# Attention's 16 own keys of each stream as a full block of 128 rows, padded with zeros

## The reference, cut to what matters

```python
ckv_all = jnp.concatenate([past_ckv.astype(c_kv.dtype), c_kv], axis=1)   # 256 + 16 keys
...
p = jax.nn.softmax(s, axis=-1).astype(v.dtype)
return jnp.einsum('bhqk,bkhd->bqhd', p, v)
```

## Time and profile before

| what | before |
|---|---|
| median of 3 runs | 1081.33 us (1079.39 to 1082.06) |
| span of the profiled execution | 1080.6 us |
| mean granted TensorE clock | 0.969 |
| PE busy | 1018.8 us (94%) |
| DVE busy | 760.0 us (70%) |
| ACT busy | 605.0 us (56%) |
| POOL busy | 82.3 us (8%) |

### The profile page before, as it was taken

How to read it: one execution, slowest core, us unless ns; L and a number is a source line. 1 busy time by engine, 2 the same in 40 slices (tenths; PEclk the granted TensorE clock), 3 DMA queues, 4 the chain that set the end, 5 groups by cost and what they waited for, 6 DMA issues and landing times.

```text
span 1080.6 us, 13540 instructions
## 1 busy us (share of the span) xinstructions
PE 1018.8 (94%) x5133; PEld 758.1 (70%) x5133; DVE 760.0 (70%) x645; ACT 605.0 (56%) x507; POOL 82.3 (8%) x109
## 2 busy tenths in 40 slices
PE   4999999999999999999969998989997989998997
PEld 4889998887666666666648686877785667766664
DVE  4456656267699888888815556662766999989896
ACT  5337432244577777777524233443536868887881
POOL 4000000004000000000021020000030000000003
PEclk9999999999999999999979999897898999999999
DMA  9542523684899999999366010303668999999984
GB/s 344 164 166 87 217 78 125 249 346 159 297 389 380 396 382 407 385 405 379 129 232 194 0 42 22 135 1 126 264 239 300 387 394 380 392 402 405 409 345 175
DMA packets 56923, 278.95 MB, mean 258 GB/s; under 512 B 6336, under 2 KB 10848, under 8 KB 48288
## 3 DMA queue, kind: packets, MB, share of 16 engines
q1 hardware_dynamic: 45424, 240.21, 57.7%
q0 software_dynamic: 8992, 29.74, 8.1%
q10 hardware_dynamic: 2464, 8.39, 2.0%
HBM read 260.45 MB, written 18.04 MB: 258 GB/s over the span
## 4 chain that ended last, share of the span: by engine, by line
PE 63%; issue 16%; DVE 8%; DMA 7%; ACT 3%; POOL 1%; ACTq 0%; SPq 0%; POOLq 0%; DVEq 0%
PE ps L189 19%; PE ps L195 9%; PE ps L527 4%; PE ps L581 4%; DMA raw<-in_moe_w_dram 4%; PE ps L624 3%; PE ps L1367 3%; PE ps L1364 3%; PE ps L2120 3%; PE ps L587 2%; PE ps L535 2%; DVE moe_wl L1104 2%; DVE raw_lo L1104 2%; PE ps L631 2%; PE ps L2095 1%
## 5 line engine op out<-in xcount | busy, mean ns | idle before, releaser
L1104 DVE TENSOR_TENSOR raw_lo<-raw,moe_wh 128x4096 fp32r<-128x4096 f32 x48 | 212.0, 4422 | 37.4 <-ACT moe_wh L1099 37.4
L1104 DVE TENSOR_TENSOR moe_wl<-moe_raw,moe_wh 128x4096 fp32r<-128x4096 f32 x48 | 212.0, 4422 | 33.6 <-ACT moe_wh L1099 33.4
L1099 ACT ACTIVATE moe_wh<-raw 128x4096 fp32r<-128x4096 f32 x48 | 174.0, 3625 | 20.8 <-DMA raw<-in_moe_w_dram 9.0
L1099 ACT ACTIVATE moe_wh<-moe_raw 128x4096 fp32r<-128x4096 f32 x48 | 173.9, 3624 | 14.1 <-DMA moe_raw<-in_moe_w_dram 14.1
L189 PE MATMUL ps<-moe_wh,moe_x 128*72 128x512 f32 x512 | 125.8, 398 | 1.7 <-DVE moe_x L1234 1.5
L189 PEld LDWEIGHTS ps<-moe_wh,moe_x 128*72 128x72 f32 x512 | 71.8, 143 | 46.0 <-DVE moe_x L1234 2.6
L329 DVE TENSOR_TENSOR raw_lo<-raw,gm_wh 128x4096 fp32r<-128x4096 f32 x12 | 53.1, 4424 | 69.6 <-ACT gm_wh L323 67.2
L189 PE MATMUL ps<-moe_wh,moe_hTh 128*72 128x512 f32 (+1 forms) x256 | 83.7, 410 | 4.9 <-DVE moe_hTl L1239 3.1
L189 PE MATMUL ps<-moe_wh,moe_hTl 128*72 128x512 f32 (+1 forms) x256 | 81.8, 401 | 0.0
L323 ACT ACTIVATE gm_wh<-raw 128x4096 fp32r<-128x4096 f32 x11 | 39.9, 3626 | 57.7 <-DMA raw<-in_gm_w_out_dram 29.2
L1364 PE MATMUL ps<-moe_wh,moe_x 128*128 128x512 f32 x224 | 58.9, 402 | 9.7 <-DVE moe_x L1234 9.7
(11 more groups left out here) (408 smaller groups left out, 1730.1 us busy)
## 6 DMA issues: line engine op xcount, KB each, us to landing
raw<-in_moe_w_dram SPq DMA_DIRECT2D x48, 2048.0 KB, 11.6
moe_raw<-in_moe_w_dram SPq DMA_DIRECT2D x48, 2048.0 KB, 11.9
raw<-in_gm_w_in_dram SPq DMA_DIRECT2D x7, 2048.0 KB, 7.9
raw<-in_gm_w_out_dram SPq DMA_DIRECT2D x4, 2048.0 KB, 7.6
moe_yrows<-moe_rows ACTq DMA_DIRECT2D x16, 288.0 KB
moe_rows<-moe_xrows POOLq DMA_DIRECT2D x14, 288.0 KB, 9.4
moe_rows<-moe_xrows POOLq DMA_DIRECT2D x14, 256.0 KB, 9.1
moe_yrows<-moe_rows ACTq DMA_DIRECT2D x14, 256.0 KB
```

The lines of the kernel that those rows point to most:

```text
L1099: nc.scalar.activation(w_hi[hi][:], w_raw[slot], ACT.Copy).then_inc(wh_ready, 1)
L1104: nc.vector.tensor_tensor(w_lo[slot], w_raw[slot], w_hi[hi][:].bitcast(F32), ALU.subtract).then_inc(wl_ready, 1)
```

## The change

`c_own` moves to partitions 112 to 127 of the same tile and gets 128 rows, of which POOL sets the first 112 to zero by a memset behind its DMAs. The third transpose turns the last 128 columns of the probabilities, that is 112 of cached keys and the 16 own ones, and ACT copies all three blocks at once. The 112 probabilities that come twice meet rows of zeros. The counts of `sm_pTc` are halved with the copies, and PE waits once for `own_zeroed`.

```diff
-        c_own = work[0:DECS, 2:4].rearrange("k a n -> k (a n)").rearrange("k (b r) -> k b r", b=DECB)
+        c_own = work[:, 2:4].rearrange("k a n -> k (a n)").rearrange("k (b r) -> k b r", b=DECB)
...
-                g.dma_start(c_own[:, b], c_sb[b * DECS:(b + 1) * DECS, SAMPLE, 0:KVR]).then_inc(ld_own, 16)
+                g.dma_start(c_own[P - DECS:P, b], c_sb[b * DECS:(b + 1) * DECS, SAMPLE, 0:KVR]).then_inc(ld_own, 16)
+            nc.gpsimd.memset(c_own[0:P - DECS], 0.0).then_inc(own_zeroed, 1)
...
-                nc.scalar.activation(psT[:, b % 2, 0:KC], ps[:, 2 + b % 2, 0:KC], ACT.Copy).then_inc(sm_pTc, 1)
-                nc.scalar.activation(psT[0:DECS, b % 2, KC:KC + P], ps[0:DECS, 2 + b % 2, KC:KC + P], ACT.Copy).then_inc(sm_pTc, 1)
+                nc.scalar.activation(psT[:, b % 2, 0:KC + P], ps[:, 2 + b % 2, 0:KC + P], ACT.Copy).then_inc(sm_pTc, 1)
...
             pe.wait_ge(ld_own, 16 * DECB)
+            pe.wait_ge(own_zeroed, 1)
...
-                    pe.wait_ge(sm_pTc, 2 * b - 2)
+                    pe.wait_ge(sm_pTc, b - 1)
...
-                nc.tensor.transpose(ps[0:DECS, 2 + b % 2, KC:KC + P], s_sb[:, b, KC:KALL], ident).then_inc(sm_pT, 1)
+                nc.tensor.transpose(ps[:, 2 + b % 2, KC:KC + P], s_sb[:, b, KALL - P:KALL], ident).then_inc(sm_pT, 1)
...
-                pe.wait_ge(sm_pTc, 2 * b + 2)
+                pe.wait_ge(sm_pTc, b + 1)
...
-                        probs = psT[0:DECS if c == 2 else P, b % 2, c * P:(c + 1) * P]
+                        probs = psT[:, b % 2, c * P:(c + 1) * P]
```

More of the change, by code:

```diff
@@ L1597, in build @@
             sem, ["sm_s", "sm_maxd", "sm_expd", "sm_p", "sm_pT", "sm_pTc", "sm_pc", "sm_pcc"])
-        sm_new, ld_own = sem("sm_new"), sem("ld_own")
+        sm_new, ld_own, own_zeroed = sem("sm_new"), sem("ld_own"), sem("own_zeroed")
         sm_o, pads_zeroed = sem("sm_o"), sem("pads_zeroed")
```

## The result

| | before | after |
|---|---|---|
| median of 6 runs each, same chip | 1080.74 us (1079.39 to 1082.20) | 1073.50 us (1072.69 to 1074.71) |
| span of the profiled execution | 1080.6 us | 1071.0 us |
| mean granted TensorE clock | 0.969 | 0.973 |

What follows compares the result with a forecast made beforehand. PE's path to the end of L2332, a gate for later loads and engines, was taken as the bound. Gaps and copy 3.0 us plus clock 1.8 gave 4.8: 1081.33 - 4.8 = 1076.5 us, range 1074.0 to 1080.5.

Steps and rivals of the forecast that it cites:

- The gaps: In values(b), changes between 16 and 128 rows cost PE 0.75 us; 1.50 us saved in streams 0, 4, 1.50 in 6, 7.
- DVE's idle time: Ahead of L1843, DVE's waits of 1.69 and 1.83 us were to fall by about 0.75 us each.
- the copy: Before values(6), ACT's one copy of 0.49 us replaces two, some 0.53 us in all: 0.04 us sooner.
- the memset: On POOL, zeroing 2048 columns on 112 partitions ends long before its first use: 0 us.
- The clock: From values(6) to the projection, a shorter stretch at half clock adds 1.8 us to the gain.
- 13.6: Length in us of the half-clock stretch before the change, 730.6 to 744.2 us, from values(6) almost to L2332.
- L: Length of the half-clock stretch after the change: expected 6.8 to 10 us, taken as 10.
- Rival 2: The half-clock stretch near stream 6 vanishes: gain 9.8 us, time 1071.5 us; chance 0.06.
- Streams 1, 2, 3 and 5 for nothing: In these streams DVE is the bound, so time saved on PE becomes idle time: 0 us.
- Rival 1: The half-clock stretch stays as long as it was: only 3.0 us gained, 1078.3 us; chance 0.20.
- rival 3: Row count doesn't matter, or time gained before L2332 is absorbed behind it: 1081.3 us; chance 0.12.
- Rival 4: The clock also falls mid-loop, a second half-clock stretch costing 6.8 us: slower, 1085.1 us; chance 0.07.

Runs made afterwards that it cites:

- the one profile with all gaps at the full clock: The kernel before with five dummy products in PE's pauses around stream 6, all gaps kept: 1081.11 us, ratio 0.9996; stage 45.4 us.
- the two later sets: Before and after measured again, no edit: 1080.61 and 1072.29 us; and once more on one chip with other variants: 1081.65 and 1074.21 us.

## Why the prediction was right in direction and wrong in size

**The gaps: right.** 0.75 us a stream were forecast for the change of row count; from the transposes of stream 0 to those of stream 1 it went from 7.21 to 6.45 us, 0.76. With 32 rows the gaps came back, with half the changes half of them went. The sum of 3.0 us at the full clock measured 3.1 in the one profile with all gaps at the full clock (45.4 - 42.3), and 2.6 by stage times clock (45.0 - 42.4, three profiles each).

**DVE's idle time, the copy, the memset: right.** DVE waited 0.92 and 1.06 us where it had waited 1.69 and 1.83; the copy takes 0.49 us and starts the products 0.04 us sooner (0.67 idle for 0.71); the memset is hidden.

**The clock: this step failed.** The prediction put the gain at 3.0 + (13.6 - L)/2 and took an L of 10, a gain of 1.8 us. The formula held: stage times clock is 44.9 to 45.0 in all three profiles of before, whatever the stretch. Its two inputs were off. What put the forecast wrong is L: it was not 10 but 0, the low stretch from stream 6 on is in none of the three profiles, and the clock took 0.0, 1.0 (43.3 - 42.3, from a stretch that began ahead of the stage) and 0.0 us. The 13.6 erred the other way, as it was one draw: in two more profiles the clock took 3.4 us of the stage, 4.5 in the mean of the three, and not 6.7. The clock's share is thus about 4.5 - 0.3 = 4.2 us where 1.8 was forecast, and with the gaps' 2.6 that is 6.8 us, the mean difference of the stages, beside the 7.2 of the first medians (and 8.3 and 7.4 of the two later sets). The 4.5 may be somewhat low, since the second and third profile are of executions 3.0 and 4.9 us below the median of their kernel, and the first of one some 1.5 above.

**Rival 2 was what happened,** at 0.06 the least likely case, and the argument against it was the wrong one: "PE's pauses ahead of values(6) become longer, not shorter". They did, and the clock stayed up. I had read the pause at 727 to 730 as the cause of the fall because it stood ahead of it; the count over all profiles says that the pause alone is not enough. Nor does every fall need one: ahead of the low stretch of the earlier trace rows PE was recorded as busy all the time, in the last 4.7 us with products of only 16 columns.

```profile
680.00:686.20 6.20, 6.20 (x59) 6.20 (x57) 4.99 (x5) 3.17 (x7) 0.00 (x0) 0.99 0.61 256
```

The rival's price was 9.8 us because it was counted from the long stretch. The two first profiles, which have just that stretch and none, do differ by 9.6 us; the medians don't.

**Streams 1, 2, 3 and 5 for nothing: only directly.** Gaps there cost no time of their own, but both profiles with gaps in these streams alone have 6.8 us at the half level in the stage, and it is 3.0 us longer in the mean, where the changed kernel lost 0.3. That gaps bring the low stretch is borne out by the count over all profiles (9 of 10 against 0 of 5). What these four streams' gaps cost in the total is likely 3 us, but not shown: two profiles, and totals whose intervals overlap.

**Rivals 1, 3 and 4 are out.** Little was absorbed behind L2332: from the projection to the end of the span the three profiles before take 333.6 us in the mean and those after 334.2. No low stretch began inside the loop of the changed kernel. The rule that rival 3 takes from the Trainium skill (TensorE: Matmul & The Clock Gate, LDWEIGHTS), that rows don't count in a weight load, isn't contradicted by a product by itself (four 16-row instructions in 0.64 us), and says nothing of what stands beside it.

**What stays open:** why the clock fell near stream 6 only where gaps and pause came together, and what decides how long it stays down. Dummies in the pauses kept the low stretch away from stream 6 in all three profiles, and in all three the routing then had 17 us at the half level, where the others have 3 to 14, mostly 10; all three are of executions 4 to 7 us above the median. Why the medians with 96 rows lie some 3 us above the changed kernel's isn't known either; one profile has 2.7 us of it ahead of the stage.

## What to carry to other kernels

Look at start-to-start distances of matmuls where the row count changes: a stage that alternates between few and many rows pays on both sides of each change, and padding with zeros, or putting the few-row products side by side, takes all or half of that away; the padding cost nothing here, as the memset is hidden. A gap on TensorE can have a second price, through the clock, which was larger here than the first. The length of a low stretch in one profile is one draw: before a gain is counted from it, profile the same kernel again, see how fast the profiled execution was among its runs, and count stage times clock.

## What the runs showed of the hardware that I had not expected

Products with 16, 32 and 64 rows next to ones with 128 show the same gaps, 96 rows none. The Trainium skill (TensorEngine Tiling (Array Packing), Tiling Modes) has modes of 32 and 64 rows and no other below 128, and says under Key Properties that a change of mode drains the engine. The runs fit that, if a product of up to 64 rows counts as such a mode, which is not shown; the price here is 0.76/4 = 0.19 us for each change at the full clock. On POOL, zeroing 112 x 2048 floats took 1.82 us, about as fast as DVE's 1.98 for 2304 columns. Executions of the kernel before, over 130 of them, spread over 10 us (1076.9 to 1087.4), the 17 of the changed one over 6 (1071.0 to 1076.7).
